# Long-convolution filter computed inside expert layer 0, its inputs loaded once in step 2, its spectra placed by quarters

## The reference, cut to what matters

```python
def _hyena_filters(L, f_w1, f_b1, f_freq, f_wi, f_bi, f_w3):
    ...
    hdn = jnp.sin(f_freq * (z @ f_w1 + f_b1))
    for n in range(HY_INNER_MLPS):                       # 2
        hdn = jnp.sin(f_freq * (hdn @ f_wi[n] + f_bi[n]))
    h = (hdn @ f_w3).astype(F32).reshape(L, HY_ORDER, 2, D)
    ...
    h = h * jnp.exp(-t[:, :, None, None] * deltas)
    kern = jnp.concatenate([h[:, :, 0], jnp.zeros((1, HY_ORDER, D), F32), jnp.flip(h[1:, :, 1], 0)], 0)
    return kern / jnp.sum(jnp.abs(kern), 0, keepdims=True)
```

## Time and profile before

| | |
|---|---|
| median of 3 runs | 1823.85 us (1821.74 to 1827.09) |
| the profiled execution | 1819.0 us, its span 1816.8 us |
| TensorE busy (matmul) | 1419.2 us, 78% |
| VectorE / ScalarE / GpSimd busy | 748.6 / 448.7 / 81.4 us |
| DMA | 504.55 MB, 278 GB/s over the span |
| mean granted clock | 0.901 |

### The profile page before, as it was taken

How to read it: one execution, slowest core, us unless ns; L and a number is a source line. 1 busy time by engine, 2 the same in 40 slices (tenths; PEclk the granted TensorE clock), 3 DMA queues, 4 the chain that set the end, 5 groups by cost and what they waited for, 6 DMA issues and landing times. The chain is left out here.

```text
span 1816.8 us, 35527 instructions
## 1 busy us (share of the span) xinstructions
PE 1419.2 (78%) x14647; PEld 788.4 (43%) x14647; DVE 748.6 (41%) x1896; ACT 448.7 (25%) x857; POOL 81.4 (4%) x109
## 2 busy tenths in 40 slices
PE   5879999999987989976465637998899985557445
PEld 2446766676666454422122213776554341222111
DVE  5767777777764366400000001767757510000001
ACT  3244565456543031110000002213121110000001
POOL 0001110111011000000000001000000000000001
PEclk8889999999997999997788769999999997878788
DMA  9023334434435499999999997224179999999995
GB/s 332 1 63 100 110 108 135 124 99 120 130 126 179 173 428 428 425 428 428 427 428 427 428 388 280 93 93 189 68 326 393 423 427 427 427 427 429 428 425 219
DMA packets 108946, 504.55 MB, mean 278 GB/s; under 512 B 16224, under 2 KB 61040, under 8 KB 83952
## 3 DMA queue, kind: packets, MB, share of 16 engines
q1 hardware_dynamic: 107520, 501.93, 69.6%
q10 hardware_dynamic: 1264, 0.33, 0.1%
HBM read 501.13 MB, written 1.09 MB: 276 GB/s over the span
## 5 line engine op out<-in xcount | busy, mean ns | idle before, releaser
L1943 PE MATMUL banks<-arena 128*32 128x512 f32 (+1 forms) x2048 | 326.7, 691 | 237.6 <-DMA arena<-in_moe_w_gate 119.1
L1943 PEld LDWEIGHTS banks<-arena 128*32 128x32 f32 (+1 forms) x2048 | 98.0, 132 | 463.7 <-issue 460.1
L2157 DVE TENSOR_TENSOR arena<-banks,arena 128x512 f32<-128x512 f32 x20 | 13.8, 692 | 632.1 <-PE banks L1943 631.8
L1953 PE MATMUL banks<-arena 128*32 128x512 f32 (+1 forms) x1024 | 148.8, 623 | 33.6 <-DMA arena<-in_moe_w_down 31.5
L797 PE MATMUL banks<-arena 128*128 128x512 f32 (+1 forms) x384 | 158.1, 550 | 0.0
L2071 ACT ACTIVATE arena<-banks,arena 128x128 f32<-128x128 f32 x80 | 30.1, 456 | 301.1 <-PE banks L1930 301.1
L1953 PEld LDWEIGHTS banks<-arena 128*32 128x32 f32 (+1 forms) x1024 | 46.4, 121 | 132.9 <-issue 125.9
L797 PEld LDWEIGHTS banks<-arena 128*128 128x128 f32 x384 | 70.2, 196 | 51.9 <-issue 43.9
L2587 PE MATMUL banks<-arena 128*128 128x256 f32 x384 | 87.4, 387 | 0.0
L2587 PEld LDWEIGHTS banks<-arena 128*128 128x128 f32 x384 | 73.7, 194 | 16.6 <-issue 6.5
L1930 PEld LDWEIGHTS banks<-arena 128*128 128x128 f32 x640 | 73.0, 192 | 16.7 <-issue 14.9
(11 more groups left out here) (412 smaller groups left out, 2323.7 us busy)
## 6 DMA issues: line engine op xcount, KB each, us to landing
arena<-in_moe_w_gate SPq DMA_DIRECT2D x64, 2048.0 KB, 25.4
arena<-in_moe_w_up SPq DMA_DIRECT2D x64, 2048.0 KB, 27.0
arena<-in_moe_w_down SPq DMA_DIRECT2D x56, 2048.0 KB, 25.3
arena<-in_ada_w SPq DMA_DIRECT2D x128, 192.0 KB, 3.0
arena<-in_ada_w SPq DMA_DIRECT2D x64, 256.0 KB, 3.6
arena<-in_moe_w_down SPq DMA_DIRECT2D x32, 512.0 KB, 16.5
arena<-in_rw_wrkv SPq DMA_DIRECT2D x24, 512.0 KB, 5.3
arena<-in_hy_w_in SPq DMA_DIRECT2D x6, 2048.0 KB, 8.9
```

Source lines behind the costliest of these rows:

```text
L1943: mm = pe.matmul(bank[j * rows:(j + 1) * rows, :], xT[:, t, j * rows:(j + 1) * rows], w[:, t], start=(t == 0), stop=(t == KT - 1), tile_po ...
L1953: mm = pe.matmul(bank[j * rows:(j + 1) * rows, :], hT[:, t, j * rows:(j + 1) * rows], w[:, k, half * 512:(half + 1) * 512], start=(t == 0) ...
L2157: dve.tensor_tensor(h, U[:, :], h, ALU.mult).then_inc(h_ready, 1)
```

## The change

The filter is computed in expert layer 0 by a new class, in 11 pieces named `FILTER_WORK`: three sine layers in gap 0 and 1 of step 3 and gap 0 of step 4, then eight units, each a quarter (256 channels) of one order, up to gap 0 of step 8. Gap 0 is before the gate product, gap 1 before the up product. Its inputs are loaded from ScalarE's queue once, at the start of step 2. For the room, slots 8 and 9 are used once only, slot 7 up to unit 29 and slot 3 up to unit 83 (`RETIRED`); in layer 1 only slot 3 is retired, and four units instead of six are loaded ahead. The spectra of the first order lie in slot 7's half block and in the columns behind the constants; the tap weights and window lie where its spectra are then written over them, quarter by quarter. `hyena_layer` loses the filter. `hyena.load_small` loses the filter's inputs; the inverse matrices (512 KB) are loaded at the start of `hyena_inputs`. Unit 0 of layer 1 is loaded at the end of `hyena_inputs`, unit 1 after the first products. The rest pass uses one block instead of three. The gathering of tokens, whose banks the filter uses, waits until the filter's last results are read.

The diff's core (places of tensors, unpacking of names and the rest pass are left out):

```diff
-FIRST_UNITS = 6
-TAIL_UNITS = 79
+LAST = 3
+RETIRED = ({WORK: 10, TAIL: 10, 7: 30, LAST: 84}, {LAST: 84})
+FIRST_UNITS = (6, 4)
...
-                if slot == TAIL and n >= TAIL_UNITS:
-                    slot = WORK
+                while n >= retired.get(slot, n + 1):
+                    slot = (slot + 1) % SLOTS_OF
...
             if not isinstance(i, int) or i > 1:
                 pe.wait_ge(y_ready, i - 1)
+            if fil is not None and isinstance(i, int):
+                fil.banks_read(pe, i - 1)
...
             for i in range(N_STEPS):
                 tokens_ready(pe, i)
+                if fil is not None and (i, 0) in FILTER_WORK:
+                    pe.wait_ge(y_ready, i)
+                    fil.multiply(pe, FILTER_WORK.index((i, 0)))
                 hidden_product(pe, i, "gate", G)
+                if fil is not None and (i, 1) in FILTER_WORK:
+                    pe.wait_ge(y_ready, i)
+                    fil.multiply(pe, FILTER_WORK.index((i, 1)))
                 hidden_product(pe, i, "up", U)
...
             for i in range(N_STEPS):
+                if fil is not None and i == 2:
+                    fil.load(act, ins)
+                if fil is not None and (i, 0) in FILTER_WORK:
+                    fil.activate(act, ins, FILTER_WORK.index((i, 0)))
                 silu_gate(act, i)
+                if fil is not None and (i, 1) in FILTER_WORK:
+                    fil.activate(act, ins, FILTER_WORK.index((i, 1)))
...
+                for gap in range(2):
+                    if fil is not None and (i, gap) in FILTER_WORK:
+                        fil.combine(dve, FILTER_WORK.index((i, gap)))
                 hidden_rows(dve, i)
...
+    def multiply(self, pe, k):
+        hy, ones = self.hy, self.s.c("ones")
+        if k:
+            pe.wait_ge(self.read, k)
...
+            q, od = self.unit(k)
+            u, at = k - SINES, slice(od * FH, (od + 1) * FH)
+            pe.wait_ge(self.hd_ready, SINES)
+            pe.wait_ge(self.f3_in, 32)
+            for i in range(TT):
+                mm = pe.matmul(self.banks[i][:, :], hy.hd[at, i * P:(i + 1) * P], hy.f_w3[at, :, q * 256:(q + 1) * 256], start=True, stop=True)
+            mm.then_inc(self.taps_done, 1)
+            pe.wait_ge(self.taps_ready, u + 1)
+            for part in range(2):
+                for i in range(TT):
+                    mm = pe.matmul(self.banks[part][:, i * 256:(i + 1) * 256], hy.fwd[part][:, i, 0:P], hy.both[:, part, i], start=True, stop=True)
+            mm.then_inc(self.spec_done, 1)
+            pe.wait_ge(self.abs_ready, u + 1)
+            for m in range(2):
+                for i in range(TT):
+                    mm = pe.matmul(self.banks[0][:, 2 * m:2 * m + 2], hy.both[:, 0, i, m * P:(m + 1) * P], ones[:, 0:2], start=(i == 0), stop=(i == TT - 1))
+            mm.then_inc(self.abs_done, 1)
...
+            if k == SINES:
+                act.wait_ge(self.delta_in, 16)
+                for i in range(TT):
+                    act.activation(hy.window[:, i], hy.window[:, 1], ACT.Exp, scale=hy.minus_t[:, i:i + 1]).then_inc(self.win_ready, 1)
+            act.wait_ge(self.spec_done, u + 1)
+            act.activation(hy.even, self.pair[:, :, 0:256], ACT.Copy).then_inc(self.even_ready, 1)
+            act.activation(hy.both, hy.both, ACT.Abs).then_inc(self.mag_ready, 1)
...
+        dve.wait_ge(self.win_ready, TT)
+        dve.wait_ge(self.taps_done, u + 1)
+        dve.tensor_tensor(h0, self.pair[:, :, 0:256], hy.window[:, :, c], ALU.mult)
+        for i in range(TT):
+            dve.scalar_tensor_tensor(h1[:, i], self.pair[:, i, 256:512], hy.keep[:, i:i + 1], hy.window[:, i, c], ALU.mult, ALU.mult)
+        dve.drain()
+        dve.tensor_tensor(hy.both[:, 0], h0, h1, ALU.add)
+        dve.tensor_tensor(hy.both[:, 1], h0, h1, ALU.subtract)
...
+        dve.wait_ge(self.even_ready, u + 1)
+        for part in range(2):
+            a, b = hy.even[:, part], self.pair[:, part, 256:512]
+            dve.tensor_tensor(hy.khat[od][part][:, 0, c], a, b, ALU.add)
...
+            dve.tensor_tensor(hy.khat[od][part][:, 1, c], first, second, ALU.subtract)
+        dve.wait_ge(self.mag_ready, u + 1)
+        dve.tensor_tensor(hy.both[:, 0], hy.both[:, 0], hy.both[:, 1], ALU.max)
...
             for n in range(BLK):
                 in_block(n)
-                if n < 2:
-                    inner_layer(n)
-                if n in taps_after:
-                    taps(taps_after.index(n))
-                if n in spectrum_after:
-                    spectrum(spectrum_after.index(n))
-                if n == BLK - 2:
-                    magnitudes()
-            turn_magnitudes()
-            pe.wait_ge(spec_ready, 4)
...
-            for n in range(2):
-                experts.load_unit(sp, ins, n, [0, 1])
+            sp.wait_ge(imag_ready, 2)
+            experts.load_unit(sp, ins, 1, [0, 1])
             sp.wait_ge(y_done, 8)
             experts.load_rows(sp, ins, mods)
-            for n in range(2, FIRST_UNITS):
+            for n in range(2, FIRST_UNITS[1]):
                 experts.load_unit(sp, ins, n, [0, 1])
```

More of the change, by code:

```diff
@@ L1695, in expert_units @@
     return units, last
-UNITS, LAST_IN = expert_units()
+UNITS, LAST_IN = zip(*(expert_units(r) for r in RETIRED))
+N_UNITS = len(UNITS[0])
 def units_of(step, kind):
-    return [n for n, unit in enumerate(UNITS) if unit[:2] == (step, kind)]
+    return [n for n, unit in enumerate(UNITS[0]) if unit[:2] == (step, kind)]
 class ExpertTensors:
@@ L1769, in load_unit @@
     def load_unit(self, sp, ins, n, of):
-        _, kind, part, cut, slot, _, _ = UNITS[n]
+        _, kind, part, cut, slot, _, _ = self.units[n]
         if cut:
@@ L1780, in weights @@
     def weights(self, n):
-        _, kind, _, cut, slot, _, _ = UNITS[n]
+        _, kind, _, cut, slot, _, _ = self.units[n]
         width = D if kind == "down" else HIDDEN
@@ L1808, in expert_layer @@
     assert s.at <= 2 * experts.large
+    s.at = experts.last
+    acc = s.take(TT, D)
+    rows_b = s.take(D)
     s.at = experts.routing
@@ L1879, in _ @@
             fixed = lambda step: [2 * step, 2 * step + 1]
-            for n in range(FIRST_UNITS, SLOTS_OF):
+            for n in range(FIRST_UNITS[experts.layer], SLOTS_OF):
                 if n == WORK:
                     sp.wait_ge(logits_done, 1)
-                experts.load_unit(sp, ins, n, fixed(UNITS[n][0]))
-            now = None
-            for n in range(SLOTS_OF, len(UNITS)):
-                step = UNITS[n][0]
+                experts.load_unit(sp, ins, n, fixed(units[n][0]))
+            now, late = None, True
+            for n in range(SLOTS_OF, N_UNITS):
+                step, used = units[n][0], units[n][6]
                 if step >= FIXED // 2 and step != now:
```

385 lines of the change are left out of this document (160 added, 225 removed).

## The result

The changed kernel takes 1834.13 us (median), the kernel before 1822.18 us in the same comparison; the ratio is 1.0055, 95% interval 1.0041 to 1.0070. It is about 10 us **slower**, where 9 us faster was forecast. The profiled execution took 1840.35 us, span 1838.5. All these starts are read from TensorE's timeline.

The account below looks back on a forecast made before the run. Bound: the weight stream in the expert layers, TensorE in the trough between. Layer 0 +17.4, trough -29.1 and layer 1 +2.5 give -9.2 us, so 1814.6 us against a median of 1823.85; range 1805 to 1834.

Parts of the forecast that it names:

- Part 1: Trough between the expert layers: with the filter gone from it, it shrinks by 29.1 us.
- Rival (e): The trough doesn't shrink because the input blocks hang on their loads: +19.9, 1843.8 us; chance 0.04.
- Part 2: Start of layer 1: four first units instead of six, the two left over partly filling a hole, +2.5 us.
- Part 3: Layer 0 with the filter and fewer slots: +15.7 to unit 35, +1.5, -4.7, +4.9, together +17.4 us.
- Neither adds to the end, because the next step is later still: Wide steps: a 4 us stream loss at unit 18 and ScalarE's 12 loads (some 5 us) don't lengthen the end.
- +1.5 us where the waits don't line up: Steps 5 to 7 with step 8's unit: TensorE's 59.1 us a step against 58.9 of stream adds 1.5 us.
- The end of the layer: Last steps of layer 0: filter constants gone -4.7 us, waits with six slots +4.9 us.
- The dry stretch of the wide steps: Layer 0's stream is dry near 717 as unit 18 waits for a slot; loses 4 us, not added to the end.
- Own case: Whole kernel: filter units of 12.6 us, products behind them 8.8, total 1814.6 us; chance 0.50 together with rival (a).
- Rival (a): Layer 0: pauses don't lower the clock, units 10.8 us, layer +12.4, total 1809.6 us; 0.50 together with own case.
- rival (b): Layer 0: low clock from the first pause, units 13.4 us, layer +30.2, total 1827.5 us; 0.22 for 1818 to 1829.
- Rival (c): TensorE bounds steps 4 to 8, taps at low clock, units 15.1 us, total 1839.4 us; 0.18 for above 1829.

Follow-up runs that it names:

- a_sp: The changed kernel with the filter's twelve loads issued on SyncE's queue ahead of unit 18 instead of ScalarE's; ratio to the kernel before 0.9996.
- a_early: The changed kernel with ScalarE issuing the filter's twelve loads one step earlier, in step 1, on its own queue; ratio to the kernel before 1.0003.
- a_later: The changed kernel with all 11 filter pieces one step later and the loads where they were; ratio to the kernel before 1.0007.
- b_ring: The kernel before with only layer 0's slots retired as in the change, the filter still between the layers; ratio to the kernel before 1.0074.
- a_sp_warm: The changed kernel with the twelve loads on SyncE's queue and three dummy matmuls in both pauses of each filter unit; ratio to the kernel before 0.9940.
- a_sp_warm1: The changed kernel with the loads on SyncE's queue and one dummy matmul in each pause of each filter unit; ratio to the kernel before 0.9960.

## Why the prediction was wrong

**Part 1 was right.** The trough lost 29.2 us for a forecast 29.1, in one run of 84.83 us. Rival (e) fell with it.

**Part 2 was right in size:** +2.7 for +2.5, of which the edit alone shows 1.6. The hole before layer 1's unit 10 is gone: from 1365 to 1385, around its first gate product, the stream runs at 429 GB/s.

**The step that failed first** is, in Part 3, the sentence "Neither adds to the end, because the next step is later still", with "first sine product 0.6" behind it in the hand-made timeline. I counted the twelve loads as bytes, 2.2 MB or 5 us, and gave them no landing time, although I had put SyncE's issue of units 18 and 19 at the very moment ScalarE issues them. They landed 33 to 50 us later, and the first sine product waited 10.69 us. It is removed by another queue (a_sp), by an earlier issue (a_early) and by later use (a_later), each time for 9 to 11 us by the ratios. That is more than half of the 19 us between forecast and result. The 5 us of bytes were too few as well: a_later, where TensorE isn't late in step 4, shows 14 us for these loads and 18.8 with the dry stretch, so the two don't stay hidden once TensorE is on time. With it gone, Part 3's own terms hold up to step 4: +15.0 measured, 15.7 forecast, and one by one too: the first unit takes 14.7 us (14.8 forecast), the product behind it 8.71 (8.8), and the down product starts 8.4 us behind the up product's end (8.2 taken for a load's landing, so the refills weren't the 1.3 us shorter of the second estimate). The table load again shows 1.28 us with the Exp right behind it (at 809.98 and 811.28 us in the changed kernel), so of the two figures for the switch the one of the rows held.

**The second step that failed** is the sum of steps 5 to 8, "+1.5 us where the waits don't line up". Its mechanism was right, the size off: the changed kernel shows +8.2 from step 4 to step 8, a_sp +10.0. I had taken 59.1 us a step, just over the stream's 58.9. The changed kernel's step 6 reads (the last row is cut short by the window's end)

```profile
905.21 7.07 PE L1963 MATMUL banks<-arena 128*32 128x512 f32 x64 [1.33 <-DMA arena<-in_moe_w_down]
...
947.67 9.77 PE L1953 MATMUL banks<-arena 128*32 128x512 f32 x64
...
965.93 1.49 PE L1963 MATMUL banks<-arena 128*32 128x512 f32 x12 [0.59 <-DMA arena<-in_moe_w_down]
```

60.7 us from down product to down product: the units 12.72 and 12.90 (25.2 taken for two, 25.6 measured), the gate and up products 8.49 and 9.77 (17.6 taken, 18.3 measured), and a wait of 0.59 for weights. No term is off by more than 0.7, but there was no slack: the step stood at the edge of the stream, and every excess counts again in each step. Against the kernel before, steps 5 to 8 took 3.0, 2.0, 0.8 and 2.4 us more. Step 8 is another case: it has one unit, and TensorE waits 8.77 us for its up weights and 4.15 for its down weights; why it takes 61.2 us all the same wasn't tried. In steps 5 to 7 the bound flips, and I had taken a middle value for the clock where the range of the rows (7.1 to 10 for a product, 10.8 to 13.4 for a unit) lay across that edge. Filling the pauses shows the other side of it: at full clock the steps are the stream's.

**The end of the layer** was forecast at +0.2 (constants -4.7, six slots +4.9); the changed kernel shows +1.6 from step 8 to the first input block. b_ring, where the constants are still there, shows +7.3, so the slots' part is some 7 rather than 4.9, and the difference, 5.7, near my 4.7 for the constants. The two errors cancel in part, and both are not far above the 1 us by which executions differ. The holes before the cut down units are there as foretold:

```profile
1151.48 1.92 PE L1963 MATMUL banks<-arena 128*32 128x512 f32 x16 [0.47 <-DMA arena<-in_moe_w_down]
1157.49 3.23 PE L1963 MATMUL banks<-arena 128*32 128x512 f32 x16 [4.08 <-DMA arena<-in_moe_w_down]
```

**The dry stretch of the wide steps** was placed rightly (near 717; found at 726 to 730 in an execution whose layer 0 starts 11.9 us later), with 4 us as its price. Alone (b_ring) it does add, 4.7 us at step 4, and in a_later it adds together with the loads; in the changed kernel it lies under TensorE's lateness, as the prediction said.

**The rivals.** Own case and (a) assumed the inputs in time. Rival (a), the full clock, is what a_sp_warm builds: units of 10.8 us, step 4 at +12.0 and the first input block at +13.2, where (a) had 10.8, +12.2 and +12.4 for layer 0. The clock fell in the first pause already, which is rival (b)'s condition; the first unit with its window takes 15.1 us (14.8 forecast), the other seven 12.5 to 14.0, 13.0 in the mean, between my 12.6 and its 13.4. (b) assumes the inputs in time and gives +3.6; a_sp, where they are, shows about 0, and for layer 0 +28.5 where (b) had +30.2. So what happened is nearest to (b), with the late inputs on top. Rival (c), which alone forecast slower than before, has the right sign and the wrong cause: its unit of 15 us and its low-clock taps (3.4 us) don't occur (the taps take 1.95 to 2.6 us, and the one unit of 15 has the window's wait in it). What made the time slower was on no rival's list, though the wait for ScalarE's loads is close to the last sentence's "a wait not seen here". By the runs' ratios: late inputs 7 to 11 us (with and without the pauses filled), low clock 10 to 13, ring alone 13.5.

## What to carry to other kernels

A load that is put beside a saturated stream has a landing time as well as bytes: look at what the other queue issues in the same microseconds, and put the load ahead of that in the same queue, or issue it while the other queue waits. Where work is fitted into an engine beside a stream, compare the sum of a step at the low clock with the stream; if it is over, filling the short pauses with dummy matmuls can decide whether the move pays: the change with both repairs is 0.6% faster than the kernel before, without them 0.55% slower.

## What the runs showed of the hardware

The four large loads of ScalarE's queue, issued within the same 9 us as units on SyncE's queue, landed after 33 to 50 us, once SyncE's six issued units were through; with no units issued beside them (a_early) they took 11 to 22 us, and on SyncE's own queue ahead of the units (a_sp) 11.8 to 15.7. How the engines choose between the two queues was not tried. The Trainium skill (DMA: Bandwidth & Descriptors, Issuing engines are not separate DMA queues) says that transfers interleave on the same engines whoever issues them, and that issuing from several saves the issue time only. The traces agree that the engines are shared, but an even interleaving would not have kept 2.27 MB waiting for 12.6 MB. The granted clock fell from 1.00 to 0.50 within a pause of 3.03 us, and around pauses of 1.98 us it fell in some units and not in others (a_sp_warm1). While the filter's loads landed, from 760 to 780 us, the DMA engines had a share of 1.00 to 1.04 and moved 8 x 315 + 8 x 246 + 4 x 255 kB, 5.5 MB, against 8.5 MB at the weights' 427 GB/s. Less the loads' own 2.27 MB that leaves 3.2 MB of the stream in 20 us, so they cost it up to 12 us where I had counted 5. The 14 us of a_later are of the same size.
